# First norm by chunks, X loaded first, sixteen modulation blocks on TensorE in column strips

## The reference

```python
mod = split(silu(c) @ w_mod[l] + b_mod[l], 6)          # shift1, scale1, gate1, shift2, scale2, gate2
mod_c = split(silu(c_ctx) @ w_mod[l] + b_mod[l], 6)    # the same for the context
hn = rms_norm(ctx, g_norm1[l]) * (1 + mod_c[1]) + mod_c[0]
xn = rms_norm(x, g_norm1[l]) * (1 + scale1) + shift1
pc, p = hn @ w_in[l], xn @ w_in[l]                     # the input product: q, k, v, fourier, conv, pool
...
four, conv, pool = fourier_mixer(p), conv_module(p), pool_mixer(p)   # conv: 31 taps over the tokens
x = x + gate1 * (concatenate([attn, four, conv, pool]) @ w_o)
x = x + gate2 * swiglu(rms_norm(x, g_norm2[l]) * (1 + scale2) + shift2)
```

## Time and profile before

| what | value |
|---|---|
| median of 3 runs | 2350.8 us (2347.71 to 2354.86) |
| profiled execution | 2349.86 us, span 2347.7 us |
| PE busy | 2205.1 us, 94% of the span |
| DVE busy | 1216.9 us, 52% |
| ACT busy | 726.0 us, 31% |
| POOL busy | 649.6 us, 28% |
| read from HBM | 209.77 MB, 90 GB/s over the span |

### The profile page before, as it was taken

The page is one execution under the profiler, slowest core; times in us unless marked ns, Lnnn a source line. Parts: engine busy times, 40 slices in busy tenths (PEclk is TensorE's granted clock), DMA queues, the critical chain, the costliest instruction groups (busy, mean ns, idle before and its releaser), DMA issues.

```text
span 2347.7 us, 26539 instructions
## 1 busy us (share of the span) xinstructions
PE 2205.1 (94%) x10994; PEld 1775.6 (76%) x10994; DVE 1216.9 (52%) x1580; ACT 726.0 (31%) x1057; POOL 649.6 (28%) x283
## 2 busy tenths in 40 slices
PE   5898897999999999799989999989999999899997
PEld 5785576888888888685668888867788888777665
DVE  5995676566556665686444213256231443511455
ACT  2323524222112221424532212222272222244532
POOL 2100002223332233200144444433234444233202
PEclk9999998999999999899999999999999999799998
DMA  7312142334333332211023323323223333221201
GB/s 260 121 46 90 37 148 68 108 126 139 104 108 126 126 125 100 67 54 72 28 77 99 117 72 99 114 66 95 76 64 94 95 99 99 63 72 52 79 1 54
DMA packets 60167, 213.59 MB, mean 91 GB/s; under 512 B 6672, under 2 KB 10384, under 8 KB 59792
## 3 DMA queue, kind: packets, MB, share of 16 engines
q1 hardware_dynamic: 57888, 206.92, 27.5%
q10 hardware_dynamic: 2160, 4.98, 0.6%
...
HBM read 209.77 MB, written 2.10 MB: 90 GB/s over the span
## 4 chain that ended last, share of the span: by engine, by line
PE 86%; DVE 8%; ACT 3%; issue 2%; DMA 1%; POOL 1%; SPq 0%; ACTq 0%; DVEq 0%
PE prod L548 73%; PE misc L586 2%; PE prod L712 1%; PE misc L648 1%; DMA ring<-in_wmod 1%; PE prod L680 1%; DVE operand_lo L1405 1%; PE prod L599 1%; PE prod L767 1%; ACT operand_hi L1036 1%; PE misc L896 1%; PE misc L791 1%; PE prod L967 1%; DVE work L1433 1%; PE misc L779 1%
## 5 line engine op out<-in xcount | busy, mean ns | idle before, releaser
L527 POOL TENSOR_TENSOR wlo<-ring,whi 128x1024 fp32r<-128x1024 f32 (+3 forms) x256 | 608.1, 2376 | 1608.4 <-ACT whi L983 1608.4
L548 PE MATMUL prod<-operand_hi,whi 128*128 128x512 f32 (+1 forms) x2208 | 734.4, 373 | 35.7 <-DVE operand_lo L1421 14.1
L548 PE MATMUL prod<-operand_hi,wlo 128*128 128x512 f32 (+1 forms) x2208 | 721.7, 367 | 0.0
L548 PE MATMUL prod<-operand_lo,whi 128*128 128x512 f32 (+1 forms) x2208 | 719.8, 366 | 0.0
L983 ACT ACTIVATE whi<-ring 128x1024 fp32r<-128x1024 f32 (+3 forms) x284 | 293.4, 1034 | 737.2 <-PE prod L548 737.2
L548 PEld LDWEIGHTS prod<-operand_hi,whi 128*128 128x128 f32 x2208 | 380.8, 190 | 124.9 <-issue 28.2
L548 PEld LDWEIGHTS prod<-operand_hi,wlo 128*128 128x128 f32 x2208 | 379.8, 190 | 68.7
L548 PEld LDWEIGHTS prod<-operand_lo,whi 128*128 128x128 f32 x2208 | 379.7, 190 | 68.5 <-issue 2.4
L1471 DVE CUSTOM_DVE_ANT_0 mod_junk<-modw,silu_c,par 128x1024 bf16<-128x1024 f32 x68 | 127.8, 1880 | 78.9 <-DMA modw<-in_wmod 78.3
L548 PE MATMUL prod<-hidden_hi,whi 128*128 128x512 f32 (+1 forms) x528 | 160.6, 358 | 0.0
L548 PE MATMUL prod<-hidden_hi,wlo 128*128 128x512 f32 (+1 forms) x528 | 160.4, 358 | 0.0
...
## 6 DMA issues: line engine op xcount, KB each, us to landing
ring<-in_w SPq DMA_DIRECT2D x224, 512.0 KB, 3.6
modw<-in_wmod SPq DMA_DIRECT2D x68, 512.0 KB, 3.7
...
ring<-in_wmod SPq DMA_DIRECT2D x28, 512.0 KB, 5.2
dft<-in_dftx SPq DMA_DIRECT2D x8, 512.0 KB, 5.7
...
```

What stands on the lines that cost most here:

```text
L527: nc.gpsimd.tensor_tensor(wlo[j % 2][:, 0:w], ring[PLACE["panel", j] % RING][:, 0:w], whi[j % 2][:, 0:w].bitcast(F32), ALU.subtract).then_ ...
L548: mm = pe.matmul(G[b][:, t0:t0 + tn], w[v][:, k * P:(k + 1) * P], a[:, t0:t0 + tn], start=(i == 0 and q == 0), stop=(i == g.kc - 1 and q = ...
```

## The change

- SP loads the parameters, then X in four quarters, then the modulation blocks; ACT issues the load of the constants; c by rows is loaded after panel 3.
- All 16 first modulation blocks are made on PE (`modulate(c)` makes block 8 + c and block c). Now silu(c), padded to 32 columns for each chunk of features, is the stationary operand and the weights move, 128 columns a matmul, in four strips of 32 columns of the array. ACT copies the four partial rows out (`mod_copy`), PE sums them and turns them with a constant `pick` of two columns, and DVE adds them to the parameters and makes the factors of one chunk (`mod_chunk`).
- PE sums the squares of every chunk (eight times L586's matmuls); POOL no longer adds.
- Panels 0 and 1 of `win0` are multiplied chunk by chunk, panel 1 two chunks behind panel 0, with `modulate(k + 3)` and `pick(k + 2)` between the chunks.
- The five later modulation blocks stand one by one among the panels (2 x 2 and one at p = 5), 12 taps move into `mixers(0)`, and the silu of c by rows is made after panel 1.

```diff
--- before.py
+++ after.py
@@ -76,8 +76,7 @@
-MOD_PE = 8
-MOD_FIRST = 16
+MOD_PE = 16
 MOD_RING = 28
@@ -85,12 +84,13 @@
...
     panels = [("panel", j) for g in GEMMS for j in range(g.j0, g.j0 + g.n)]
-    first = [("mod", k // 2 + MOD_PE * (1 - k % 2)) for k in range(MOD_FIRST)]
-    order = first + panels[:2]
-    for i in range(4):
-        order += [("mod", MOD_FIRST + k) for k in ((0, 1), (2,), (3,), (4,))[i]] + [panels[2 + i]]
+
+    first = [("mod", k // 2 + DC * (1 - k % 2)) for k in range(MOD_PE)]
+    order = first[:6] + panels[:2] + first[6:] + panels[2:4]
+    for i in range(5):
+        order += [("mod", MOD_PE + i), panels[4 + i]]
     cut = GEMM["wout0"].j0 + 2
-    return order + panels[6:cut] + [("mod", k) for k in range(MOD_FIRST + 5, MOD_RING)] + panels[cut:]
+    return order + panels[9:cut] + [("mod", k) for k in range(MOD_PE + 5, MOD_RING)] + panels[cut:]
@@ -432,9 +436,9 @@
...
         def _(sp):
-            sp.dma_start(silu_c[:, :], d["c"]).then_inc(c_landed, 16)
             sp.dma_start(par[:, :], d["par"]).then_inc(par_landed, 16)
-            sp.dma_start(con[:, :], d["con"]).then_inc(par_landed, 16)
+            for s in range(4):
+                sp.dma_start(X[:, 2 * s:2 * s + 2, :], d["xt"][:, 2 * s:2 * s + 2, :]).then_inc(x_landed[s], 16)
@@ -444,7 +448,7 @@
...
                 elif i < MOD_PE:
-                    sp.wait_ge(shift_used, i + 1)
+                    sp.wait_ge(shift_used, 2 * (i % DC) + 2 - i // DC)
                 else:
@@ -468,15 +472,14 @@
...
-            for r in range(RING // 2):
-                load_mod(ORDER[r][1])
-            sp.dma_start(X[:, :, :], d["xt"]).then_inc(x_landed, 16)
             own = MOD_RING
-            for kind, j in ORDER[RING // 2:]:
+            for kind, j in ORDER:
                 if kind == "mod":
...
                 load_panel(j)
+                if j == 3:
+                    sp.dma_start(silu_c[:, :], d["c"]).then_inc(c_landed, 16)
                 for l in range(2):
@@ -502,11 +505,6 @@
...
         def _(pool):
-            for c in range(1, DC):
-                pool.wait_ge(square_ready, c + 1)
-                wait(pool, square_added, c - 1)
-                nc.gpsimd.tensor_tensor(W[1][:, :], W[1][:, :], W[0][:, :], ALU.add).then_inc(square_added, 1)
-
@@ -823,20 +821,57 @@
...
-            pe.wait_ge(c_ready, 1)
-            for k in range(MOD_PE):
-                landed(pe, ("mod", k))
-                w = ring[PLACE["mod", k] % RING]
-                for c in range(DC):
-                    mm = pe.matmul(M0[:, 2 * k:2 * k + 2], w[:, c * P:(c + 1) * P], silu_cp[:, 2 * c:2 * c + 2],
-                                   start=(c == 0), stop=(c == DC - 1))
-                mm.then_inc(shift_used, 1)
+            def modulate(c):
+
+                bank = (M1, MM)[c % 2]
+                wait(pe, mod_read, c - 1)
+                for q in (1, 0):
+                    landed(pe, ("mod", DC * q + c))
+                    w = ring[PLACE["mod", DC * q + c] % RING]
+                    for i in range(DC):
+                        g = 32 * (i % 4)
+                        mm = pe.matmul(bank[g:g + 32, P * q:P * q + P], silu_cp[:, 32 * i:32 * i + 32], w[:, i * P:(i + 1) * P],
+                                       start=(i < 4), stop=(i >= 4))
+                    mm.then_inc(shift_used, 1)
+
+            def pick(c):
+
+                pe.wait_ge(mod_copied, c + 1)
+                for q in range(2):
+                    mm = pe.matmul((M1, MM)[c % 2][:, 256 + 2 * q:258 + 2 * q], mod_rows[c % 2][:, P * q:P * q + P], co("pick"),
+                                   start=True, stop=True)
+                mm.then_inc(mod_picked, 1)
+
+            def first_panels(p, k):
+                def ready(k):
+                    if k % 2:
+                        pe.wait_ge(odd_lo, k // 2 + 1)
+                    else:
+                        pe.wait_ge(operand_lo, k + 1)
+                panel("win0", p, xh, xl, NT, k, k + 1, ready=ready)
+
+            pe.wait_ge(con_landed, 16)
+            sum_squares(DC, NT, W, out=F[:, 0:8])
+            pe.wait_ge(pad_ready, 1)
+            modulate(0)
+            modulate(1)
+            pick(0)
+            spread_roots(NT, W)
+            modulate(2)
+            pick(1)
+            for k in range(DC + 2):
+                if k < DC:
+                    first_panels(0, k)
+                if k > 1:
+                    first_panels(1, k - 2)
+                if k + 3 < DC:
+                    modulate(k + 3)
+                if k + 2 < DC:
+                    pick(k + 2)
...
                 width, segs = tok(l)
-                if l == 0:
-                    rms(1, NT, W, free=lambda: pe.wait_ge(shift_read, 1), total=W[1])
-                else:
+                if l == 1:
                     rms(1, NT, W, total=fh)
@@ -851,7 +886,8 @@
...
-                big(f"win{l}", xh, xl, lambda p, l=l: win_width(l, p), ready=OPS[f"win{l}"], after=qk_norm, panels=12)
+                big(f"win{l}", xh, xl, lambda p, l=l: win_width(l, p), ready=OPS[f"win{l}"], after=qk_norm, panels=12,
+                    begin=0 if l else 2)
                 mixers(l)
@@ -1021,11 +1057,20 @@
...
+            def mod_copy(c):
+                act.wait_ge(shift_used, 2 * c + 2)
+                wait(act, mod_picked, c - 1)
+                nc.scalar.activation(mod_rows[c % 2][:, :], (M1, MM)[c % 2][:, 0:256], ACT.Copy).then_inc(mod_copied, 1)
+
             def norm_mod(l, which, width):
-                root(width, 1024)
-                if l == 0 and which == 0:
+                first = l == 0 and which == 0
+                root(width, 1024, source=F[:, 0:8] if first else None)
+                if first:
+                    mod_copy(0)
                     high(0)
+                    mod_copy(1)
                     high(1)
+                    mod_copy(2)
                 for c in range(DC):
@@ -1036,6 +1081,8 @@
...
                     ins.then_inc(operand, 1)
+                    if first and c + 3 < DC:
+                        mod_copy(c + 3)
@@ -1154,17 +1201,16 @@
...
-            act.wait_ge(par_landed, 32)
-            nc.scalar.activation(silu_cp[:, :], pa("c"), ACT.Silu)
-            act.wait_ge(c_landed, 16)
-            nc.scalar.activation(silu_c[:, :], silu_c[:, :], ACT.Silu).then_inc(c_ready, 1)
-            act.wait_ge(x_landed, 16)
+            act.dma_start(con[:, :], d["con"]).then_inc(con_landed, 16)
+            act.wait_ge(par_landed, 16)
+            act.wait_ge(pad_cleared, 1)
+            nc.scalar.activation(silu_cp[:, :].rearrange("p (c s) -> p c s", c=DC)[:, :, 0:2],
+                                 pa("c").rearrange("p (c s) -> p c s", c=DC), ACT.Silu).then_inc(pad_ready, 1)
+            rms([X[:, c, 0:NT] for c in range(DC)], NT, W, lambda c: act.wait_ge(x_landed[c // 2], 16))
+            act.wait_ge(con_landed, 16)
...
                 width, segs = tok(l)
-                if l == 0:
-                    for c in range(DC):
-                        square(c, X[:, c, 0:NT], NT, W[0], W[1], lambda c: None)
                 norm_mod(l, 0, NT)
@@ -1186,6 +1232,9 @@
                 def qk_norm(p, l=l):
+                    if l == 0 and p == 1:
+                        act.wait_ge(c_landed, 16)
+                        nc.scalar.activation(silu_c[:, :], silu_c[:, :], ACT.Silu).then_inc(c_ready, 1)
                     if 5 <= p <= 8:
@@ -1408,7 +1457,16 @@
...
-            def norm_mod(l, which, width):
+            def mod_chunk(c):
+
+                both = pa("mod0")[:, 0:4 * DC].rearrange("p (b c s) -> p c b s", b=2, c=DC)[:, c]
+                dve.wait_ge(mod_picked, c + 1)
+                nc.vector.tensor_tensor(both, both, (M1, MM)[c % 2][:, 256:260].rearrange("p (b s) -> p b s", b=2),
+                                        ALU.add).then_inc(mod_read, 1)
+                dve.wait_ge(mod_read, c + 1)
+                link(nc.vector.tensor_scalar(afac[:, c:c + DC + 1:DC], both[:, 1], 1.0, pa("g10")[:, c:c + 1], ALU.add, ALU.mult))
+
+            def norm_mod(l, which, width, before=None):
                 r = invert(width, W)
@@ -1623,22 +1683,13 @@
...
-            dve.wait_ge(par_landed, 32)
-            dve.wait_ge(c_ready, 1)
-            for k in range(MOD_PE, MOD_FIRST):
-                ring_mod(k)
-            dve.wait_ge(shift_used, MOD_PE)
-            shift = pa("mod0")[:, 0:2 * MOD_PE]
-            nc.vector.tensor_tensor(shift, shift, M0[:, 0:2 * MOD_PE], ALU.add).then_inc(shift_read, 1)
-            dve.wait_ge(shift_read, 1)
-            dve.wait_ge(mod_step, mods_done(MOD_FIRST - 1))
-            n["squared"] += DC
-            n["added"] += DC - 1
-            modulation(0, 0)
-            dve.wait_ge(x_landed, 16)
+            nc.vector.memset(silu_cp[:, :], 0.0).then_inc(pad_cleared, 1)
+            dve.wait_ge(par_landed, 16)
+            for s in range(4):
+                dve.wait_ge(x_landed[s], 16)
             for l in range(2):
```

(24 more changed lines are left out.)

16 lines of the change are left out of this document (11 added, 5 removed).

## The result

The changed kernel takes 2379.0 us (median of 5, 2377.2 to 2382.7), the kernel before 2354.2 (median of 5, 2347.7 to 2363.8). The ratio is 1.0103, 95% interval 1.0081 to 1.0124: 1% slower, 25 us by the medians. The forecast was 2365.

What follows compares the result with a forecast made beforehand. After its start the kernel was taken as a row of TensorE matmuls (86% of the chain). From 2349.9, a mark 11.9 us later (43 + 46.5 + 8 = 97.5 against 85.65) plus 3.0 gave 2364.8; range 2346 to 2388.

Steps and rivals of the forecast that it cites:

- round trip: Loop of panels 0 and 1: no chunk's operand made before the previous product; 7.0 us odd, 5.5 even at first.
- The base: Starting time of the sum: the profiled execution of the kernel before, 2349.9 us, with a median of 2350.8.
- To the first product: Start, from column sums ending at 27.8: first chunk of the product ends at 43 (41 to 46).
- ACT is not later: Before the first product: panel 0 loads in 3.6 us, ACT's high(0) ends near 36.3, chunk 1's copy at 36.7.
- The strips: Modulation blocks in four column strips: 0.037 us a pass, 1.2 us for a chunk's two blocks at the fast clock.
- The loop at 2.4 GHz: Panels 0 and 1 after the first product chunk, to the end of panel 1, at fast-clock prices: 46.5 us.
- The clock in the loop: Panels 0 and 1: three tenths of PE's 27 us of work charged as slow, 8 us.
- From there a panel takes 8.32 us: Panels of win0 after the mark at panel 1's end: 8.32 us each, 1.04 us for each of eight chunks.
- "3 us" for the mean: First mixer, pair 4: PE's mean waits for four convolution taps moved there, 3 us that nothing downstream absorbs.
- the one with the clock up in the column sums: Rival at the start: PE reaches 2.4 GHz 4 us into the sums; mark at 80, time 2347; chance 13%.
- the second rival: Strips dear (0.074 or 0.124 us a pass) or the clock low throughout the loop: 2372 to 2400; chance 22%.
- The loop with the clock high: Rival in panels 0 and 1: same loop without the 8 us, time 2357, or 2351 with cheaper strips; chance 18%.

Runs made afterwards that it cites:

- e11: The changed kernel with GpSimd's low part of panel 1 held until VectorE has made chunk 0's low operand: 2377.8 us, one execution.
- e4: The changed kernel with 28 or 18 extra unread PE matmuls ahead of panel 0's products of chunks 1 to 6: 2370.9 us, ratio 1.0066.
- e3: The changed kernel with the four taps of pair 4 moved back into panels 7 to 10 of win0: 2374.1 us, ratio 1.0077.
- e8: The changed kernel with the edits of e1 and e3, and a block's matmuls reordered so two in a row share a column strip: 2346.6 us, one execution.
- e9: The changed kernel with the edits of e1 and e3, and ten extra 256-column matmuls ahead of the first column sum: 2339.1 us, one execution.
- e1: The changed kernel with PE's modulate(k+3) and pick(k+2) put ahead of the product of chunk k: 2351.3 us, ratio 0.9984.

## Why the prediction was off

The direction and the main mechanisms were right: slow column sums, cheap strips, a first product at 43.2 ("near 40", and 41.2 in the working), a round trip with holes of 3.87 us (odd, "about 4") and 2.75 (even, "2"), a mean that waits 3.56 ("3"). The sizes were not. The step of the working that failed most is the price of a hole on PE: the mean was charged its wait alone, 3 us, and cost 5.7, and the low clock in the loop was charged 8 us and cost 10.5. Against 2365 the median is 14 us more, and the steps are these.

- *The base, 4.3 us.* The sum was made on one execution of 2349.9 and the median of the three then known, 2350.8. The median of five is 2354.2.
- *To the first product, 2.4 us* (45.4 for "43"). The picks were done at 38.7 ("38.5"), but that is luck. The strips were 1 us cheaper than forecast, and "ACT is not later" was wrong: panel 0's load took 5.27 us instead of 3.6, so ACT's high part began at 36.34, where it should have ended, and pick(1) waited 1.37 us for the copy behind it. The product itself took 2.2 us instead of 1.8 (twice the 1.04 would have been 2.1). The rest is DVE: its two small operations at "0.4" took 1.1 and the low operand at "1.15" took 2.13, while POOL's low parts of panels 0 and 1 ran beside them. The prices were read in the earlier trace rows, where POOL was idle beside them; e11 shows the cause. The Trainium skill (Trainium Architecture — The Big Picture, What this means for kernel authors) says that VectorE and GpSimd share one pair of SBUF ports, under an exclusive lock. The 2.13 us beside GpSimd in the changed kernel, against 1.14 in e11, agrees.
- *The strips.* "1.2 us" for a chunk's two blocks is 1.08 (1.94 at the low clock): 0.034 a pass, midway between two strips squared (0.037) and the bound at a quarter of full width (0.031).
- *The loop at 2.4 GHz.* "46.5 us" stands: 40.9 against 40.5 for the part that e4 shows.
- *The clock in the loop: 10.5 us for "8".* The loop took 57.05 us, 46.5 and 10.5. I took three tenths of PE's work as slow, between two rows of the trace before. The loop took 10.5 over its price at 2.4 GHz, nearer to four tenths: PE waits ahead of six of the seven products that follow the first, and the mean granted clock was 0.84, 0.72 and 0.91 already inside the holes at 47.8, 66.0 and 75.4. e4 gives 9.9 us of the 10.5 by itself.
- *"From there a panel takes 8.32 us".* 8.53 in the changed kernel, and as much in e3, e8 and e11, 0.9 us in all. That is 0.355 us for each of 24 pairs of matmuls instead of 0.347. The other runs lose at most 0.3 us over the four panels. The cause is open.
- *"3 us" for the mean: 5.7.* The wait itself was right. What was missing is that this hole also brings the low clock for what comes behind it, here 2.05 us on the mean alone (e3). I had charged the clock in the loop, and not here.

The terms add up to 4.3 + 2.4 + 2.5 + 0.9 + 2.7 = 12.8 of the 14; the rest is within what medians of five tell (the five times of the kernel before lie 16 us apart).

Of the rivals, the one with the clock up in the column sums fell: 96 passes ran at 0.215 us to the end, and e9 shows that even a raised clock does not last in them. The Trainium skill (TensorE: Matmul & The Clock Gate, Part 1) describes the clock as released by sustained matmul activity. In e9 PE was busy without a gap when it fell, so the page's rule does not cover one-column matmuls. The measured time lies in the second rival's 2372 to 2400, but not for its reasons: the strips took 0.034 a pass, and the clock was 0.71 in the loop and not low throughout. The loop with the clock high is what e4 made by force: its gain shows that 2351 to 2357 had asked for a PE without holes.

What the prediction did not ask is whether the order could be otherwise. It named the cause (the copy of chunk c+3 ahead of operand_hi, the modulation behind the product), and exactly that edit, e1, takes back 27.7 us.
